# Reordering the products inside score and value groups of a two-part hybrid model on one core

## What is computed

```python
# first block, branch B: scores of one head times decays, then times the values
scores = einsum('bhctd,bhcsd->bhcts', q, k) * exp(d_log - m_t[..., None])   # d = 64
num = einsum('bhcts,bhcse->bhcte', scores, v) + ...
# second block: stick-breaking attention, head dimension 128
z = einsum('bthd,bshd->bhts', qb, kb) * scale
log_beta = log_sigmoid(z)
log_1m_beta = where(causal, log_beta - z, 0.0)
after = cumsum(log_1m_beta, axis=3, reverse=True) - log_1m_beta
weights = where(causal, exp(log_beta + after), 0.0)
out = einsum('bhts,bshe->bthe', weights, vb)
```

## Time and profile before

| | us |
|---|---|
| median of 3 runs | 3241.22 (3240.91 to 3242.47) |
| the profiled execution's own time | 3241.84 |
| its span in the profile | 3240.1 |
| TensorE busy | 3210.5 (99%) |
| weight loads busy | 2689.5 (83%) |
| GpSimd busy | 2067.3 (64%) |
| VectorE busy | 1373.7 (42%) |
| ScalarE busy | 830.1 (26%) |

### The profile page before, as it was taken

The page is one execution under the profiler, slowest core; times in us unless marked ns, Lnnn a source line. Parts: engine busy times, 40 slices in busy tenths (PEclk is TensorE's granted clock), DMA queues, the critical chain, the costliest instruction groups (busy, mean ns, idle before and its releaser), DMA issues.

```text
span 3240.1 us, 49284 instructions
## 1 busy us (share of the span) xinstructions
PE 3210.5 (99%) x15796; PEld 2689.5 (83%) x15796; DVE 1373.7 (42%) x2205; ACT 830.1 (26%) x1813; POOL 2067.3 (64%) x2052
## 2 busy tenths in 40 slices
PE   7999999999999999999999999999999999999999
PEld 6888888887888888888888888888888888888887
DVE  6767652236666542255554213111365552132121
ACT  5555340025554420022221002011222220021021
POOL 5555657765556567766656776766665567766665
PEclk9999999999999999999999999999999999999999
DMA  3322222232222222322222232222322222222222
GB/s 121 91 87 83 91 84 91 97 103 77 91 85 91 84 85 97 105 96 82 88 87 78 97 104 90 95 95 97 108 84 86 81 73 96 97 98 97 98 97 98
DMA packets 89648, 298.33 MB, mean 92 GB/s; under 512 B 12592, under 2 KB 13488, under 8 KB 89552
## 3 DMA queue, kind: packets, MB, share of 16 engines
q1 hardware_dynamic: 74592, 271.61, 25.4%
q10 hardware_dynamic: 14960, 25.40, 2.6%
HBM read 282.23 MB, written 2.13 MB: 88 GB/s over the span
## 4 chain that ended last, share of the span: by engine, by line
PE 96%; DVE 1%; DMA 1%; POOL 1%; issue 0%; ACTq 0%; ACT 0%; DVEq 0%; SPq 0%; POOLq 0%
PE bank L566 30%; PE bank L568 30%; PE bank L567 29%; PE bank L671 2%; PE bank L728 1%; PE bank L783 1%; PE bank L704 1%; PE bank L717 1%; PE bank L816 1%; PE bank L666 0%; DMA raw<-in_w_in 0%; PE bank L680 0%; POOL w_lo L550 0%; DVE xn L1483 0%; PE bank L683 0%
## 5 line engine op out<-in xcount | busy, mean ns | idle before, releaser
L550 POOL TENSOR_TENSOR w_lo<-raw,w_hi 128x512 fp32r<-128x512 f32 x1024 | 1385.6, 1353 | 85.4
L547 POOL TENSOR_SCALAR w_hi<-raw 128x512 fp32r<-128x512 f32 x1024 | 699.4, 683 | 1064.8 <-DMA raw<-in_w_in 724.3
L566 PE MATMUL bank<-h_lo,w_hi 128*128 128x512 f32 (+1 forms) x2912 | 1128.4, 387 | 3.9 <-POOL w_lo L550 3.7
L568 PE MATMUL bank<-h_hi,w_hi 128*128 128x512 f32 (+1 forms) x2912 | 1114.9, 383 | 0.0
L567 PE MATMUL bank<-h_hi,w_lo 128*128 128x512 f32 (+1 forms) x2912 | 1113.3, 382 | 0.0
L566 PEld LDWEIGHTS bank<-h_lo,w_hi 128*128 128x128 f32 x2912 | 548.3, 188 | 108.5 <-POOL w_lo L550 4.9
L568 PEld LDWEIGHTS bank<-h_hi,w_hi 128*128 128x128 f32 x2912 | 547.8, 188 | 108.0
L567 PEld LDWEIGHTS bank<-h_hi,w_lo 128*128 128x128 f32 x2912 | 548.5, 188 | 102.1
L1505 DVE TENSOR_TENSOR x<-x,bank 128x512 f32<-128x512 f32 x64 | 44.0, 688 | 391.8 <-PE bank L568 391.6
L566 PE MATMUL bank<-w_lo,up_hi 128*128 128x512 f32 x512 | 199.5, 390 | 0.0
L568 PE MATMUL bank<-w_hi,up_hi 128*128 128x512 f32 x512 | 199.2, 389 | 0.0
(11 more groups left out here) (285 smaller groups left out, 4268.9 us busy)
## 6 DMA issues: line engine op xcount, KB each, us to landing
raw<-in_w_in SPq DMA_DIRECT2D x288, 512.0 KB, 3.3
raw<-in_w_up SPq DMA_DIRECT2D x64, 512.0 KB, 3.3
raw<-in_w_down SPq DMA_DIRECT2D x64, 512.0 KB, 3.2
raw<-in_w_out_a SPq DMA_DIRECT2D x16, 512.0 KB, 3.3
raw<-in_w_out_b SPq DMA_DIRECT2D x16, 512.0 KB, 3.3
raw<-in_w_o SPq DMA_DIRECT2D x16, 512.0 KB, 3.2
raw<-in_p_ret SPq DMA_DIRECT2D x16, 512.0 KB, 3.2
raw<-in_p_sb SPq DMA_DIRECT2D x16, 512.0 KB, 3.2
```

Source lines behind the costliest of these rows:

```text
L547: nc.gpsimd.tensor_scalar(m.w_hi[:, slot, w], m.raw[:, slot, w], 1.0, 0.0, ALU.mult, ALU.add).then_inc(s["w_step"], 1)
L550: nc.gpsimd.tensor_tensor(m.w_lo[:, slot, w], m.raw[:, slot, w], m.w_hi[:, slot, w].bitcast(F32), ALU.subtract).then_inc(s["split"], 1)
L566: nc.tensor.matmul(dst, hi, rhs_lo, start=first, stop=False, **more)
L568: return nc.tensor.matmul(dst, hi, rhs_hi, start=False, stop=last, **more)
```

## The change

Three functions of TensorE's program and the list of `pair_of_heads` change. The number and the shapes of the products stay the same, as does what every other engine does.

- `m_scores` gets the blocks that it is to make. The first head makes blocks 3, 2, 1, then come the value turns of the second head, and block 0 (512 columns) follows with the grant `bs_done`. The second head makes 3, 2, 1, 0.
- `z_scores` makes in each group high times low, then the mask, then low times high and high times high.
- `s_values` makes the first two products of block 0, then blocks 1 to 3, and ends with block 0's high times high.

```diff
-            def m_scores(a):
+            def m_scores(a, blocks):
                 if a == 0:
                     pe.wait_ge(s["bqk_ready"], at.at("pair", 1, times=2))
                 r = slice(64 * a, 64 * a + 64)
-                for sb in range(TB):
+                for sb in blocks:
...
-                mm.then_inc(s["bs_done"], 1)
+                if blocks[-1] == 0:
+                    mm.then_inc(s["bs_done"], 1)
...
-                    product(zt[qb], m.stq_hi[:, tok], m.stq_lo[:, tok], m.stk_hi[:, 0:n], m.stk_lo[:, 0:n],
-                            True, False, skip_group_check=True)
-                    mm = nc.tensor.matmul(zt[qb][:, qb * P:n], m.ident_b[:], m.mx_b[:], start=False, stop=True,
-                                          skip_group_check=True)
+                    more = dict(skip_group_check=True)
+                    nc.tensor.matmul(zt[qb], m.stq_hi[:, tok], m.stk_lo[:, 0:n], start=True, stop=False, **more)
+                    nc.tensor.matmul(zt[qb][:, qb * P:n], m.ident_b[:], m.mx_b[:], start=False, stop=False, **more)
+                    nc.tensor.matmul(zt[qb], m.stq_lo[:, tok], m.stk_hi[:, 0:n], start=False, stop=False, **more)
+                    mm = nc.tensor.matmul(zt[qb], m.stq_hi[:, tok], m.stk_hi[:, 0:n], start=False, stop=True, **more)
...
-                for sb in range(TB):
-                    n = S - sb * P
-                    w = slice(SOFF[sb], SOFF[sb] + n)
-                    mm = product(m.bank[5][:, sb * P:S], m.sv_hi[:, sb], m.sv_lo[:, sb], m.sw_hi[:, w],
-                                 m.sw_lo[:, w], sb == 0, sb == TB - 1)
-                mm.then_inc(s["so_done"], 1)
+                whole = slice(SOFF[0], SOFF[0] + S)
+                so = m.bank[5]
+                nc.tensor.matmul(so[:], m.sv_hi[:, 0], m.sw_lo[:, whole], start=True, stop=False)
+                nc.tensor.matmul(so[:], m.sv_lo[:, 0], m.sw_hi[:, whole], start=False, stop=False)
+                for sb in range(1, TB):
+                    w = slice(SOFF[sb], SOFF[sb] + S - sb * P)
+                    product(so[:, sb * P:S], m.sv_hi[:, sb], m.sv_lo[:, sb], m.sw_hi[:, w], m.sw_lo[:, w],
+                            False, False)
+                nc.tensor.matmul(so[:], m.sv_hi[:, 0], m.sw_hi[:, whole], start=False,
+                                 stop=True).then_inc(s["so_done"], 1)
...
                     m_value_turns(0)
-                    m_scores(0)
+                    m_scores(0, (3, 2, 1))
                     m_value_turns(1)
+                    m_scores(0, (0,))
                     h_gemm()
                     m_values(0)
-                    m_scores(1)
+                    m_scores(1, (3, 2, 1, 0))
```

## The result

| | before | after |
|---|---|---|
| median of the runs beside each other, us | 3241.53 (3240.06 to 3243.14, 8 runs) | 3251.69 (3248.16 to 3253.32, 8 runs) |
| the profiled execution's own time, us | 3241.84 | 3248.16 |
| its span, us | 3240.1 | 3246.3 |

The ratio is 1.0029 with a 95% interval of 1.002 to 1.0038: 6.5 to 12.3 us slower. The forecast was 3248.9, and its range ended at 3251.2. So the sign is as forecast and the loss somewhat larger, with the median 0.5 above the range. The profiled execution itself is 6.3 longer than the one before, less than the 7.7 of the sum.

What follows compares the result with a forecast made beforehand. TensorE, busy 99% of the span, was taken as the bound. Terms 7.4 + 0.4 - 0.3 + 0.2 = 7.7 us on the profiled 3241.84 made 3249.5, or 3248.9 for a median 0.6 below; range 3245.0 to 3251.2.

Steps and rivals of the forecast that it cites:

- Part 1: First head of each pair: turns wait for copied vTb, two more row changes; loss 0.92, eight times, 7.4 us.
- The load behind a long product: Row change after a 512-column product: next load 0.37 after its start (bounds 0.23 to 0.43), 16 times.
- 0.14 beyond the work: At row changes, the next load comes 0.14 after the array finishes the last product; assumed behind long products too.
- The rival that a long product hides the change: Row change behind a long product: load at 0.23 gives 3246.7, at 0 gives 3244.9; chance 0.14.
- Part 2: Second head, order 128, 256, 384, 512, no new row change: loss 0.04 to 0.05, eight times, 0.4 us.
- blocks 256 and 384 together last 0.87: Step for the second head's scores: duration of these two blocks, taken from the old profile (366.36 to 367.23).
- Part 3: Mask products in stick-breaking scores: the gap moves with the mask, 64 masks without gain; 0.3 us gained at 128-column groups.
- this exception: 128-column stick-breaking group: mask could load after 0.06 instead of 0.12, 16 times, 0 to 1.0 us gained, 0.3 taken.
- Part 4: Stick-breaking values ending with a long product: 0 to 0.05 lost ahead of output turns, eight times; 0.2 us taken.
- The later grant: bs_done, granted some 1.1 later in the first head; VectorE's decay products stay covered by another panel, 5.4.
- the rival that would have cost 8 us: Values of the first head: later bs_done makes TensorE wait, 1 us per pair, 8 us, 3257; chance 0.07.

Runs made afterwards that it cites:

- e4: Kernel before, first head split: blocks 0, 1, 2, then second head's turns, then block 3; second head as before: 3245.69 against 3241.61 us, ratio 1.0014.
- e6: Changed kernel with decay scores on all 128 rows (sum of both heads' scores), so without row changes: 3241.83 us against 3241.52 before, ratio 1.0002.
- e5: Kernel before, its order kept, decay scores on all 128 rows (sum of both heads' scores), so no row changes: 3237.34 against 3241.52 us, ratio 0.9988.
- e3: Kernel before with decay scores in order 3, 2, 1, 0 in both heads, in one piece ahead of the turns: 3242.15 against 3241.61 us, ratio 1.0001.
- e2: Kernel before with only masks second in their groups and values ending with block 0's last product: 3240.61 against 3241.61 us, ratio 0.9996.
- e9: Kernel before with zero-padded 128-row keys (second head's made later), masks second, values ending with their long product: 3239.58 against 3242.34 us, ratio 0.9993.
- e11: Changed kernel, unaltered, one more profiled execution: 3251.07 us.
- e1: Kernel before with only the decay scores in the changed order, masks and values as before: 3250.61 against 3241.61 us, ratio 1.0027.
- e10: Changed kernel, unaltered, timed again beside the kernel before: 3251.65 against 3241.09 us, ratio 1.0033; its profile 3249.87.
- e12: Changed kernel, unaltered, another profiled execution: 3249.25 us.

## Why the prediction was right, and where it was off

**Part 1, the wait of the turns: right, nearly to the hundredth.** Turns' load 2.36 behind the first turn (forecast 2.37), load behind the turns 0.58 later (0.59), third long product 0.57 later (0.57), load behind it 0.33 (0.37), panel's second product 0.33 later (0.34): 4.17 instead of 4.24. Over eight pairs 7.08 instead of 7.4. That both causes are needed is shown by e4 (row changes nearly without the wait, 4.1) and by e6 against e5 (the wait without row changes, 4.5).

**The load behind a long product: right kind, size a little high.** "0.14 beyond the work" became 0.09 to 0.10 (0.32 or 0.33, less 0.23). Sixteen times that is 0.7 less than forecast, and this is the term of the sum that was sized too high. The rival that a long product hides the change is refuted by this row and by e3. (The range was said to take in this rival; its edge, 3245.0, takes in the figure 3246.7 and not 3244.9.) The Trainium skill (page "TensorE: Matmul & The Clock Gate", section "Step-by-step: what each phase is for") has loads pulled ahead of matmuls in flight when row groups do not conflict or they target the background; read so that every load is pulled ahead, this gave 3244.9, and the traces disagree at every change of rows, behind a short and behind a long product alike, and agree where the rows stay equal (e5).

**Part 2, the second head: 0.07 instead of 0.04 to 0.05.** The step that was off is "blocks 256 and 384 together last 0.87". In ascending order they take 0.93 (367.72 to 368.65): the first 256-column product behind the short ones is followed after 0.17 and not 0.12. The smaller row change gave 0.05 of this back, and the second panel product came 0.02 later, so 2.46 instead of 2.43. In sum 0.58 instead of 0.4.

**Part 3, the masks: right.** The load waits for the end of the product ahead, wherever the mask stands. The group of 128 columns has its mask 0.06 to 0.07 earlier, and that group is 0.06 shorter (1475.59 to 1475.94, before 1469.22 to 1469.63), so this exception was real; the stretches of scores and values together show no more than 0.3 saved over the run, and e2 and e9 show nothing that can be told from no change.

**Part 4, the values: right.** The stretch ahead of the output turns is 0.03 longer, 0.26 over the eight times, with 0.2 forecast.

**The later grant: no wait.** TensorE does not wait for the decayed scores anywhere in the changed kernel, so the rival that would have cost 8 us is out.

**What was missing.** The sum had no term for the clock. I counted what the new wait costs by itself, and not what a TensorE with holes in it may be granted afterwards. The traces show up to 3.2 us of this in one execution. It may be what put the median 0.5 above the range; that is not shown. The profiled execution of the first series, with no such stretch, came out 1.3 below the forecast sum on its basis (3249.5 against 3248.16): its pairs lost 7.7, and the rest of it is 1.5 shorter than in the profile before, most of it in the waits at the norms (4.7 against 6.5). That the pairs come out at 7.7 beside the 7.8 of parts 1 and 2 is closer than the terms are: part 1 was 0.3 too high and part 2 was 0.2 too low, and it is luck that they offset each other.

## What to carry to other kernels

On an engine that is busy 99% of the time, look at what an order puts between a helper's copy and its use: moving 0.7 us of work from ahead of a wait to behind it cost 0.4 us a pair at once, and in some executions more in the clock. Do not cut a run of products on 64 rows in two; each change between 64 and 128 rows cost 0.1 to 0.2 us, whatever the last product's length, and padding to 128 rows takes it away if the engine that fills the padding has room at that very place. When a change adds short waits to a saturated TensorE, take several profiles and look at the granted clock behind each.

## What the runs showed of the hardware

- Among these float32 products a weight load begins with the product ahead (300.09 beside 300.08) while the rows stay the same. At a change between 64 and 128 rows it comes 0.19 to 0.20 after the start of a 128-column product and 0.32 to 0.33 after that of a 512-column one. All four changes of a pair together are worth 0.5 us (e5, 4.2 over eight pairs); the two of a second head are worth 0.33.
- Products on all 128 rows cost no more than on 64: in e5 512 columns follow at 0.23 and 128 columns at 0.11, as before.
- A bfloat16 load between float32 products on the same rows is not pulled ahead: it stands 0.23 to 0.24 behind the start of a 512-column product, at either place in the group.
- The clock fell to its lower level behind waits of only 0.36 to 0.41 us, which were followed by a row change, three products and another row change (469.11 to 470.58 in e11), each time at a cost of 1.6 us. It did so at four of the 40 such places in the five profiles with this order and row changes (changed kernel, e1, e10, e11, e12).
